# Expert blocks activated into a ring in SBUF, and latents normalised ahead of the logarithm

## The chip, the cores and the metric

The kernel runs on 1 core of one Trainium2 chip. The metric is the time of the device in microseconds (us) from start to end of one execution. A core has five engines that run side by side, each through its own queue in order: TensorE (PE, matrix products into PSUM), VectorE (DVE), ScalarE (ACT), GpSimd (POOL), and SyncE (SP), which here only issues DMAs. They wait for one another through counts (semaphores).

## The reference

Two layers of a trunk, 640 tokens (128 of context, 512 of a sample) of width 1024. What matters here, cut down:

```python
h = rmsnorm(x, norm1_g) * (1 + sc1) + sh1
(mq, mk, mv, mo, gates..., cu, cv, cq, ckv, kr) = split_cols(h @ w_in)
ml_out = ...                                   # mLSTM both ways; log_sigmoid of the forget gates
cm_out = cu * (ws @ rmsnorm(cv, cm_norm_g) + bs)          # spatial gating
q = rmsnorm(cq, mla_q_norm_g) @ mla_w_uq                   # latents, normalised
ckv_n = rmsnorm(ckv, mla_kv_norm_g)
att = attention(q, ckv_n @ mla_w_ukv, rotary keys, cached context)
x = x + g1 * (concat(ml_out, cm_out, att) @ w_out)
h2 = rmsnorm(x, norm2_g) * (1 + sc2) + sh2
# PEER: 8 heads choose 16 of 16384 single-neuron experts by product keys
act = gelu(einsum('thkd,td->thk', u_tab[eidx], h2))
x = x + g2 * einsum('thk,thkd->td', softmax(sc) * act, v_tab[eidx])
```

## The kernel before, in words

The loop over the two layers runs five stages one after the other: the input projection (`project`), the mixers (`mix`), the choice of experts (`retrieve`), the gate matrices (`gate_matrices`) and the experts (`experts`). The order on each engine is written out by hand; nothing is scheduled automatically. Products in full precision are made from a high and a low part (`_hi`, `_lo`), three passes each: ScalarE makes the high part by a copy that rounds, VectorE or GpSimd the low part by a subtraction.

**Experts.** The 640 tokens are treated in two ways. For tokens of tiles 0 and 1 the chosen rows of both tables are gathered (L1644, 1 MB each, 256 in a layer) into a ring of 6 places; VectorE takes a dot product (`dot`, L1988), ScalarE its gelu and its share (L1899, L1907), VectorE adds the weighted row (`weigh`, L1998) and frees the place (`row_used`). For the other 384 tokens all 16384 experts are computed densely in 128 blocks of 128: 116 of them (`DIRECT`) here in full, the hidden values of the last 12 earlier. For block i TensorE makes the hidden products (`hidden`, L1849, 24 matmuls) into PSUM bank i % 2, ScalarE takes the gelu in place there (L1922), VectorE multiplies by the gate block in place (`gate`, L1973), ScalarE copies the high part (`high_a`, L1913), VectorE subtracts for the low part (`low_a`, L1977), and TensorE makes the output products (`outputs`, L1860, 18 matmuls). u and v come as pairs of blocks by SP's DMAs, issued when VectorE has made u_lo (L1954, `u_split`) and v_lo (L1981, `v_split`); the gate blocks are fetched on the count `gated`.

TensorE's order is hidden(i+2), outputs(i), hidden(i+3), and so on. hidden(i+2) writes the bank of block i and so waits for `a_ready` of block i, which low_a gives; it also waits for `u_split`. VectorE's order in block i is gate(i), dots, low_u(i+2), one weigh, low_a(i), the other weighs, low_v(i), a last dot. ScalarE's is gelu(i), activations of the rows of block i-1, high_u(i+2), their shares, high_a(i), high_v(i).

**Mixers.** SP issues 3 small loads (count `rows_load`) and then 10 more (`b_load`, normg among them). VectorE first makes the gate rows r_i, r_f and r_e (L1024 to L1027), which release ScalarE's exponential and logarithm (L917, L919), then the rotary keys, then waits for `b_load` and normalises cv, cq and ckv (L1037, L1040). TensorE transposes cq and ckv (L694), ScalarE copies them (L924, L925), and then come the gating products (L701), the products of q (L710), their copies, the exponentials of the rows (L934) and the transposes of the rows into columns (L720), which VectorE copies (L1097). On VectorE the chain from the logarithm (L1044 on, scans over time) ends ahead of L1084.

**Gate matrices.** VectorE, GpSimd and ScalarE make one-hot rows by comparing `iota` with the chosen keys, TensorE multiplies them (L1712). `iota` is loaded at the start of the stage (count `e_load`), in each layer.

Of the kernel before, what the change touches and what calls it, by code (L numbers as in the profile page):

```python
# [105 lines left out]
def build_program(nc, a, o):  # L106
# [14 lines left out]
    eps_col = sb("eps_col", [P, 1])  # L121
    one_col = sb("one_col", [P, 1])
# [195 lines left out]
    with nc.Block() as block:  # L318
        @block.sync
        def _(sp):  # L320
            sp.dma_start(c_rows[:, :, :], a["c"].partition_broadcast(P)).then_inc(c_load0, 16)
            for i in range(len(FIRST) - 1):
# [12 lines left out]
            sp.wait_ge(load, 64)  # L335
# [3 lines left out]
        def _(dve):  # L339
# [11 lines left out]
            dve.wait_ge(load, 64)  # L351
# [199 lines left out]
    b_load = K.sem("b_load")  # L551
    c_load = K.sem("c_load")
# [63 lines left out]
    def mix(l):  # L616
# [29 lines left out]
        with nc.Block() as block:  # L646
            @block.sync
            def _(sp):
                sp.dma_start(cos_sin[HD:QK, :, :], a["cos_sin"]).then_inc(rows_load, 16)
                sp.dma_start(cos_sin[QK:P, 1, :], a["cos_sin"][:, 1, :]).then_inc(rows_load, 16)  # L650
                sp.dma_start(gate_b[:, :], a["gate_b"][l]).then_inc(rows_load, 16)
                loads = [(normg[:, :, :], a["normg"][l].partition_broadcast(P)), (m0[:, :], a["m0"][l]), (sel8[:, :, :], a["sel8"]),
# [29 lines left out]
            def _(pe):  # L682
# [14 lines left out]
                pe.wait_ge(b_load, 16 * 10)  # L697
# [210 lines left out]
            def _(act):  # L908
# [7 lines left out]
                act.wait_ge(nf_ready, 1)  # L916
                act.activation(r_e[:, :], r_e[:, :], ACT.Exp).then_inc(log_ready, 1)  # L917
                act.wait_ge(log_ready, 1)
                act.activation(r_e[:, :], r_e[:, :], ACT.Ln, bias=1.0).then_inc(log_ready, 1)  # L919
                act.wait_ge(b_load, 16 * 10)  # L920
                for t in range(NT):
# [5 lines left out]
                                   ACT.Copy).then_inc(lat_taken, 1)  # L927
                for h in range(AH):
# [84 lines left out]
            def _(dve):  # L1013
# [7 lines left out]
                link(dve.memset(r_m[:, :], 0.0))  # L1021
                dve.wait_ge(rows_load, 48)
# [12 lines left out]
                dve.wait_ge(b_load, 16 * 10)  # L1035
                dve.wait_ge(root15, 1)
                link(dve.reciprocal(rstd[:, 0:15], rstd[:, 0:15]))  # L1037
                for t in range(NT):
                    for i, c in enumerate((CV, CQ, CKV)):
                        ins = dve.scalar_tensor_tensor(pj(t, c), pj(t, c), rstd[:, 3 * t + i:3 * t + i + 1],  # L1040
                                                       normg[:, i, :], ALU.mult, ALU.mult)
                    ins.then_inc(normed, 1)
# [1144 lines left out]
```

## Time and profile before

| | us |
|---|---|
| median of 3 runs | 3939.42 (3938.99 to 3949.62) |
| the profiled execution, its own time | 3980.82 |
| its span | 3979.0 |
| TensorE busy | 3625.8 (91%) |
| VectorE busy | 3403.8 (86%) |
| ScalarE busy | 1483.8 (37%) |
| GpSimd busy | 1267.3 (32%) |
| mean DMA rate | 262 GB/s over the span |

Busy time is what an engine spends in instructions that the profiler records; the rest is waiting. In the profile a wait is put down to what released it last: `a <- b` says that a waited until b was done. The share of busy time is a mean over stages with different limits, so a stage has to be read for itself. The experts of the first layer lie between some 937 and 2015 us of the span, those of the second between some 2884 and 3956.

### The profile page before, as it was taken

The numbers are of one execution on the slowest core, as the hardware profiler recorded it, in microseconds if no ns is written. First come the engines' busy times: TensorE is split into PE (matmuls) and PEld (weight loads), VectorE is DVE, ScalarE is ACT, GpSimd is POOL, SyncE is SP. The second block draws the span as 40 slices with busy tenths as digits, with TensorE's granted clock in tenths as the row PEclk, the third lists the DMA queues.
The fourth block names the chain that finished last, engine by engine and source line by source line (L and its number), as shares of the span: only waits on it lengthen the run. The fifth ranks groups of instructions, "written<-read, shape, count | busy, mean of one in ns | idle before, by whom it ended". The sixth has DMA issues, their size and how long they took to land. (4 is left out here: it accounts for less than half of the span.)

```text
span 3979.0 us, 58872 instructions
## 1 busy us (share of the span) xinstructions
PE 3625.8 (91%) x19804; PEld 3185.2 (80%) x19804; DVE 3403.8 (86%) x7095; ACT 1483.8 (37%) x3422; POOL 1267.3 (32%) x1008
## 2 busy tenths in 40 slices
PE   4979989988999999999978899898889999999996
PEld 4947779667889888888778578895788888888885
DVE  8964657997999999999979557599989999999997
ACT  3331232185334343433343322323834343333343
POOL 0000023094443433444300001223934444444441
PEclk9975899999999999999989779898999999999998
DMA  6710021257999999999946101114599999999996
GB/s 243 229 60 23 1 76 59 72 211 269 405 413 414 402 403 400 403 398 399 402 142 227 43 22 54 45 47 168 194 373 399 408 406 405 406 402 400 403 411 249
DMA packets 205909, 1043.35 MB, mean 262 GB/s; under 512 B 19193, under 2 KB 74041, under 8 KB 103297
## 3 DMA queue, kind: packets, MB, share of 16 engines
q1 hardware_dynamic: 131970, 504.00, 33.3%
q0 software_dynamic: 73728, 536.90, 32.9%
q8 instruction: 88, 1.44, 0.1%
q14 instruction: 123, 1.01, 0.1%
HBM read 982.56 MB, written 58.27 MB: 262 GB/s over the span
## 5 line engine op out<-in xcount | busy, mean ns | idle before, releaser
L1644 POOL DMA_INDIRECT held_rows<-in_uv_rows,chosen x428 | 744.4, 1739 | 1169.6 <-DVE y L1998 1044.2
L1849 PE MATMUL ps<-hd_hi,u_hi 128*128 128x384 f32 x1856 | 640.8, 345 | 78.6 <-DVE a_lo L1977 67.9
L1849 PE MATMUL ps<-hd_hi,u_lo 128*128 128x384 f32 x1856 | 629.4, 339 | 0.0
L1849 PE MATMUL ps<-hd_lo,u_hi 128*128 128x384 f32 x1856 | 629.2, 339 | 0.0
L1988 DVE CUSTOM_DVE_ANT_0 held_rows<-held_rows,h2rows 128x1024 f32<-128x1024 f32 x428 | 520.7, 1218 | 67.6 <-DMA held_rows<-in_uv_rows,chosen 67.6
L1998 DVE SCALAR_TENSOR_TENSOR y<-held_rows,shares_now,y 128x1024 f32<-128x1024 f32 x428 | 545.3, 1277 | 0.0
L1899 ACT ACTIVATE acts<-dots 128x1 f32<-128x1 f32 x512 | 97.8, 195 | 1159.9 <-DVE dots L1988 1159.4
L1860 PE MATMUL ps<-v_hi,a_hi 128*128 128x512 f32 x1536 | 479.6, 394 | 14.1 <-DVE a_lo L1977 8.7
L1860 PE MATMUL ps<-v_lo,a_hi 128*128 128x512 f32 x1536 | 475.8, 391 | 0.0
L1860 PE MATMUL ps<-v_hi,a_lo 128*128 128x512 f32 x1536 | 474.8, 390 | 0.0
L1849 PEld LDWEIGHTS ps<-hd_hi,u_hi 128*128 128x128 f32 x1856 | 351.2, 189 | 119.5 <-issue 69.7
L1849 PEld LDWEIGHTS ps<-hd_lo,u_hi 128*128 128x128 f32 x1856 | 351.6, 189 | 5.1
L1849 PEld LDWEIGHTS ps<-hd_hi,u_lo 128*128 128x128 f32 x1856 | 351.5, 189 | 0.0
L1860 PEld LDWEIGHTS ps<-v_lo,a_hi 128*128 128x128 f32 x1536 | 289.8, 189 | 63.5
L1860 PEld LDWEIGHTS ps<-v_hi,a_lo 128*128 128x128 f32 x1536 | 289.7, 189 | 61.1
L1860 PEld LDWEIGHTS ps<-v_hi,a_hi 128*128 128x128 f32 x1536 | 285.5, 189 | 62.2 <-issue 15.5
L1981 DVE TENSOR_TENSOR v_lo<-v_raw,v_hi 128x1024 fp32r<-128x1024 f32 x256 | 311.9, 1219 | 12.0 <-ACT v_hi L1893 11.8
L1954 DVE TENSOR_TENSOR u_lo<-u_raw,u_hi 128x1024 fp32r<-128x1024 f32 x232 | 283.1, 1221 | 26.7 <-ACT u_hi L1888 26.7
L1893 ACT ACTIVATE v_hi<-v_raw 128x1024 fp32r<-128x1024 f32 x256 | 268.6, 1049 | 67.7 <-PE ps L1860 52.7
L1009 POOL TENSOR_TENSOR wout_lo<-wout_even,wout_hi 128x2048 fp32r<-128x2048 f32 x4 | 18.3, 4576 | 854.7 <-ACT wout_hi L989 854.7
L1712 PE MATMUL ps<-hot 128*128 128x128 f32 x1536 | 223.5, 292 | 44.8 <-POOL hot L1698 25.6
L1888 ACT ACTIVATE u_hi<-u_raw 128x1024 fp32r<-128x1024 f32 x232 | 242.7, 1047 | 37.0 <-DMA u_raw<-in_u 33.8
(316 smaller groups left out, 7448.0 us busy)
## 6 DMA issues: line engine op xcount, KB each, us to landing
v_raw<-in_v SPq DMA_DIRECT2D x128, 1024.0 KB, 9.0
u_raw<-in_u SPq DMA_DIRECT2D x116, 1024.0 KB, 13.6
mod_ring<-in_ada SPq DMA_DIRECT2D x96, 512.0 KB, 4.1
gates_dram<-gmat SPq DMA_DIRECT2D x12, 4096.0 KB, 13.7
gt<-gates_dram SPq DMA_DIRECT2D x64, 768.0 KB, 12.3
wq<-in_wq SPq DMA_DIRECT2D x8, 2048.0 KB, 8.2
ahead_raw<-in_u SPq DMA_DIRECT2D x24, 512.0 KB, 4.0
w_odd<-in_w_in SPq DMA_DIRECT2D x8, 1024.0 KB, 5.4
```

The lines of the kernel that those rows point to most:

```text
L1009: pool.tensor_tensor(wout_lo[:, c % 2, :, :], wout[c % 2], wout_hi[:, c % 2, :, :], ALU.subtract).then_inc(wout_split, 1)
L1644: pool.indirect_dma_start(picked(n).rearrange("p a d -> p (a d)"), None, a["uv_rows"], bass.IndirectOffsetOnAxis(ap=chosen[:, n % GT, n // ...
L1712: ins = pe.matmul(ps[:, q % 8, r * P:(r + 1) * P], hot2[:, s, r, :], hot1[:, s, r, :], start=True, stop=True)
L1849: ins = pe.matmul(ps[:, b % 2, 0:TD], (u_hi, u_lo)[wl][:, b % 2, k, :], (hd_hi, hd_lo)[hl][:, k, :], start=(k == 0 and n == 0), stop=(k == ...
L1860: ins = pe.matmul(ps[:, 2 + 2 * t + half, :], (a_hi, a_lo)[al][:, b % 4, t * P:(t + 1) * P], (v_hi, v_lo)[vl][:, b % 2, half * 512:(half + ...
L1888: act.activation(u_hi[:, b % 2, :, :], u_raw[:, b % 4, :, :], ACT.Copy).then_inc(u_high, 1)
L1893: act.activation(v_hi[:, b % 2, :], v_raw[:, b % 4, :], ACT.Copy).then_inc(v_high, 1)
L1899: act.activation(acts[:, i % COLS, t:t + 1], dots[:, i % COLS, t:t + 1], ACT.Gelu_apprx_tanh).then_inc(dot_act, 1)
L1954: dve.tensor_tensor(u_lo[:, b % 2, :, :], u_raw[:, b % 4, :, :], u_hi[:, b % 2, :, :], ALU.subtract).then_inc(u_split, 1)
L1981: dve.tensor_tensor(v_lo[:, b % 2, :], v_raw[:, b % 4, :], v_hi[:, b % 2, :], ALU.subtract).then_inc(v_split, 1)
L1988: dve.tensor_tensor_reduce(row, row, h2rows[:, t, :], 1.0, 0.0, ALU.mult, ALU.add, dots[:, i % COLS, t:t + 1]).then_inc(dot_ready, 1)
L1998: dve.scalar_tensor_tensor(to, picked(n)[:, 1, :], shares_now[:, i % COLS, t:t + 1], to, ALU.mult, ALU.add).then_inc(row_used, 1)
```

## The change

Three edits. (1) The gelu of a block goes from PSUM into `active`, a ring of four places in SBUF, where gate, high_a and low_a then work. The PSUM bank is free once the gelu is done, so hidden(i+2) waits for `hid_act` and no longer for `a_ready`. The rings of a_hi and a_lo shrink from four places to two, and high_a(i) waits for outputs(i-2). On ScalarE gelu(i+1) is issued in block i, ahead of the rows' activations. (2) In the mixers normg is loaded first, on a count of its own (`normg_load`), and VectorE normalises the latents ahead of the gate rows; ScalarE's exponential and logarithm stand behind its latent copies. (3) `iota` is loaded once at the start and kept; the constants eps_col and one_col share one tensor.

```diff
+    eps_one = sb("eps_one", [P, 2])
+    eps_col, one_col = eps_one[:, 0:1], eps_one[:, 1:2]
+    iota = sb("iota", [P, NKEYS])
...
+                    sp.dma_start(iota[:, :], a["iota"]).then_inc(load, 16)
...
+                sp.dma_start(normg[:, :, :], a["normg"][l].partition_broadcast(P)).then_inc(normg_load, 16)
                 sp.dma_start(cos_sin[HD:QK, :, :], a["cos_sin"]).then_inc(rows_load, 16)
...
-                loads = [(normg[:, :, :], a["normg"][l].partition_broadcast(P)), (m0[:, :], a["m0"][l]), (sel8[:, :, :], a["sel8"]),
+                loads = [(m0[:, :], a["m0"][l]), (sel8[:, :, :], a["sel8"]),
...
-                act.wait_ge(nf_ready, 1)
-                act.activation(r_e[:, :], r_e[:, :], ACT.Exp).then_inc(log_ready, 1)
-                act.wait_ge(log_ready, 1)
-                act.activation(r_e[:, :], r_e[:, :], ACT.Ln, bias=1.0).then_inc(log_ready, 1)
-                act.wait_ge(b_load, 16 * 10)
+                act.wait_ge(b_load, 16 * 9)
                 for t in range(NT):
                     act.wait_ge(lat_psum, t + 1)
...
+                act.wait_ge(nf_ready, 1)
+                act.activation(r_e[:, :], r_e[:, :], ACT.Exp).then_inc(log_ready, 1)
+                act.wait_ge(log_ready, 1)
+                act.activation(r_e[:, :], r_e[:, :], ACT.Ln, bias=1.0).then_inc(log_ready, 1)
...
-                dve.wait_ge(b_load, 16 * 10)
+                dve.wait_ge(normg_load, 16)
                 dve.wait_ge(root15, 1)
                 link(dve.reciprocal(rstd[:, 0:15], rstd[:, 0:15]))
...
-                sp.dma_start(iota[:, :], a["iota"]).then_inc(e_load, 16)
...
-    a_hi = sb("a_hi", [P, 4, TD], F32R, stack=s9)
-    a_lo = sb("a_lo", [P, 4, TD], F32R, stack=s9)
+    a_hi = sb("a_hi", [P, 2, TD], F32R, stack=s9)
+    a_lo = sb("a_lo", [P, 2, TD], F32R, stack=s9)
+    active = sb("active", [P, 4, TD], stack=s9)
...
                     if not isinstance(g, int) or g * BODY + b >= 2:
-                        pe.wait_ge(a_ready, g * BODY + b - 1)
+                        pe.wait_ge(hid_act, g * BODY + b - 1)
...
                 def high_a(g, b):
                     act.wait_ge(gated, g * BODY + b + 1)
-                    act.wait_ge(out_psum, g * BODY + b + 1)
-                    act.activation(a_hi[:, b % 4, :], ps[:, b % 2, 0:TD], ACT.Copy).then_inc(a_high, 1)
+                    act.wait_ge(out_psum, g * BODY + b + 3)
+                    act.activation(a_hi[:, b % 2, :], active[:, b % 4, :], ACT.Copy).then_inc(a_high, 1)
+
+                def gelu(i):
+                    act.wait_ge(hid_psum, i + 3)
+                    if i >= 4:
+                        act.wait_ge(a_ready, i - 3)
+                    act.activation(active[:, i % 4, :], ps[:, i % 2, 0:TD], ACT.Gelu_apprx_tanh).then_inc(hid_act, 1)
 
                 high_u(0, 0)
                 high_u(0, 1)
+                gelu(0)
                 for i in range(NKEYS):
                     g, b = i // BODY, i % BODY
                     before = rows_of(i - 1) if i >= 1 else ()
-                    if i < DIRECT:
-                        act.wait_ge(hid_psum, i + 3)
-                        act.activation(ps[:, b % 2, 0:TD], ps[:, b % 2, 0:TD], ACT.Gelu_apprx_tanh).then_inc(hid_act, 1)
-                    else:
+                    if i + 2 < DIRECT:
+                        high_u(g, b + 2)
+                    if i + 1 < DIRECT:
+                        gelu(i + 1)
+                    if i >= DIRECT:
                         high_v(g, b)
                     for n in before:
                         row_activation(n)
-                    if i + 2 < DIRECT:
-                        high_u(g, b + 2)
                     for n in before:
                         row_share(n)
                     high_a(g, b)
...
-                    to = ps[:, b % 2, 0:TD]
+                    to = active[:, i % 4, :]
```

How the order changes on ScalarE in the experts: one block of the steady part, first before, then after. u_hi is high_u of block i+2, shares_now the shares, a_hi and v_hi the high parts, and the instruction that reads ps (L1922, then L1919) the gelu.

```order
408 L1907 ACTIVATE shares_now<-acts,gates 128x1 x2
409 L1913 ACTIVATE a_hi<-ps 128x384
410 L1893 ACTIVATE v_hi<-v_raw 128x1024
411 L1922 ACTIVATE ps<-ps 128x384
412 L1899 ACTIVATE acts<-dots 128x1 x2
413 L1888 ACTIVATE u_hi<-u_raw 128x1024
```

```order
408 L1899 ACTIVATE acts<-dots 128x1 x2
409 L1907 ACTIVATE shares_now<-acts,gates 128x1 x2
410 L1913 ACTIVATE a_hi<-active 128x384
411 L1893 ACTIVATE v_hi<-v_raw 128x1024
412 L1888 ACTIVATE u_hi<-u_raw 128x1024
413 L1919 ACTIVATE active<-ps 128x384
```

Before, the gelu (L1922) stood ahead of the activations of the rows (L1899) and u_hi behind them; now u_hi and the gelu (L1919), which is that of the following block, both stand ahead of them, and with them ahead of the shares and a_hi.

On ScalarE at the start of the mixers, first before, then after; rowq is the row r_e, under L917/L919 (then L929/L931) the exponential and the logarithm, cqT and ckvT the latent copies, qT those of q.

```order
70 L917 ACT_TABLE_LOAD
71 L917 ACTIVATE rowq<-rowq 36x640
72 L919 ACT_TABLE_LOAD
73 L919 ACTIVATE rowq<-rowq 36x640
74 L924 ACTIVATE cqT<-ps 128x2x128
75 L925 ACTIVATE ckvT<-ps 128x2x128
```

```order
78 L924 ACTIVATE cqT<-ps 128x2x128
79 L925 ACTIVATE ckvT<-ps 128x2x128
80 L929 ACT_TABLE_LOAD
81 L929 ACTIVATE rowq<-rowq 36x640
82 L931 ACT_TABLE_LOAD
83 L931 ACTIVATE rowq<-rowq 36x640
84 L935 ACTIVATE qT<-ps 128x512
```

The two table loads and the two activations went from ahead of the five tiles' copies to behind them, directly ahead of the copies of q.

On VectorE at the same place, first before, then after; proj_b are the latents and cv, krT and xn the rotary keys, the first rowq rows r_i, r_f and r_e, and the last one (L1044, then L1049) the first step behind the logarithm.

```order
302 L1024 TENSOR_SCALAR rowq<-smallT,gate_b 36x640
303 L1025 TENSOR_SCALAR rowq<-smallT,gate_b 36x640
304 L1027 SCALAR_TENSOR_TENSOR rowq<-rowq 36x640
305 L1030 COPY krT<-smallT 32x128
306 L1031 TENSOR_TENSOR krT<-smallT,cos_sin 32x512
307 L1032 TENSOR_TENSOR xn<-smallT,cos_sin 32x512
308 L1033 TENSOR_TENSOR krT<-krT,xn 32x512
309 L1037 RECIPROCAL rstd<-rstd 128x15
310 L1040 SCALAR_TENSOR_TENSOR proj_b<-proj_b,rstd,normg 128x256 x15
311 L1044 SCALAR_TENSOR_TENSOR rowq<-rowq 36x640
```

```order
302 L1028 RECIPROCAL rstd<-rstd 128x15
303 L1031 SCALAR_TENSOR_TENSOR proj_b<-proj_b,rstd,normg 128x256 x15
304 L1036 TENSOR_SCALAR rowq<-smallT,gate_b 36x640
305 L1037 TENSOR_SCALAR rowq<-smallT,gate_b 36x640
306 L1039 SCALAR_TENSOR_TENSOR rowq<-rowq 36x640
307 L1042 COPY krT<-smallT 32x128
308 L1043 TENSOR_TENSOR krT<-smallT,cos_sin 32x512
309 L1044 TENSOR_TENSOR xn<-smallT,cos_sin 32x512
310 L1045 TENSOR_TENSOR krT<-krT,xn 32x512
311 L1049 SCALAR_TENSOR_TENSOR rowq<-rowq 36x640
```

The reciprocal and the fifteen normalisations went from behind the gate rows and the keys to ahead of them; the step behind the logarithm stays at row 311.

## Rows read from the trace of the kernel before

**Rows 1.** Waits of TensorE, whole span: us in total, times, longest

```profile
PE ps L1849 <- DVE a_lo L1977: 67.9, 62, 10.3
...
PE ps L694 <- DVE proj_b L1040: 13.9, 2, 7.0
```

**Rows 2.** Windows, first layer's experts: us, busy per engine, clock, DMA share, GB/s

```profile
930.00:1950.00 1020.00, 977.82 (x4873) 880.37 (x4871) 953.23 (x1210) 397.31 (x961) 411.68 (x248) 0.99 0.98 397
...
1340.00:1440.00 100.00, 98.58 (x492) 88.43 (x491) 96.36 (x123) 40.77 (x100) 39.70 (x25) 1.00 1.01 412
```

**Rows 3.** Waits of VectorE from 930 to 1950 us

```profile
DVE held_rows L1988 <- DMA held_rows<-in_uv_rows,chosen: 35.9, 29, 2.7
...
DVE u_lo L1954 <- ACT u_hi L1888: 13.6, 6, 4.5
```

**Rows 4.** Timeline, VectorE, one block: start, us, engine, line, operation

```profile
1203.58 0.56 DVE L1973 TENSOR_TENSOR ps<-ps,gt 128x384 f32<-128x384 f32 x1
...
1205.19 1.22 DVE L1954 TENSOR_TENSOR u_lo<-u_raw,u_hi 128x1024 fp32r<-128x1024 f32 x1
...
1206.32 1.27 DVE L1998 SCALAR_TENSOR_TENSOR y<-held_rows,shares_now,y 128x1024 f32<-128x1024 f32 x1
...
1207.52 0.55 DVE L1977 TENSOR_TENSOR a_lo<-ps,a_hi 128x384 fp32r<-128x384 f32 x1
...
1211.46 0.56 DVE L1973 TENSOR_TENSOR ps<-ps,gt 128x384 f32<-128x384 f32 x1
```

**Rows 5.** Timeline, TensorE, beside it: first instructions of three groups

```profile
1205.06 0.63 PE L1860 MATMUL ps<-v_hi,a_hi 128*128 128x512 f32 x2
...
1209.16 0.34 PE L1849 MATMUL ps<-hd_hi,u_hi 128*128 128x384 f32 x1
...
1213.37 0.63 PE L1860 MATMUL ps<-v_hi,a_hi 128*128 128x512 f32 x2
```

**Rows 6.** Timeline, ScalarE, the same block

```profile
1204.75 0.46 ACT L1907 ACTIVATE shares_now<-acts,gates 128x1 f32<-128x1 f32 x2
...
1206.43 0.48 ACT L1922 ACTIVATE ps<-ps 128x384 f32<-128x384 f32 x1
```

**Rows 7.** Timeline, three engines, at the first expert blocks

```profile
958.85 0.66 PE L1849 MATMUL ps<-hd_hi,u_hi 128*128 128x384 f32 x1 [10.29 <-DVE a_lo L1977]
...
963.91 1.28 DVE L1998 SCALAR_TENSOR_TENSOR y<-held_rows,shares_now,y 128x1024 f32<-128x1024 f32 x1
...
965.36 0.47 ACT L1922 ACTIVATE ps<-ps 128x384 f32<-128x384 f32 x1 [1.23 <-PE ps L1849]
```

**Rows 8.** Timeline, VectorE, at the start of the mixers

```profile
217.82 0.25 DVE L1037 RECIPROCAL rstd<-rstd 128x15 f32<-128x15 f32 x1 [2.20 <-DMA krT<-in_kr_cacheT]
...
218.11 6.03 DVE L1040 SCALAR_TENSOR_TENSOR proj_b<-proj_b,rstd,normg 128x256 f32<-128x256 f32 x15
...
224.05 0.81 DVE L1044 SCALAR_TENSOR_TENSOR rowq<-rowq 36x640 f32<-36x640 f32 x1
...
236.55 3.92 DVE L1084 SCALAR_TENSOR_TENSOR mixed<-ps,cmb,proj_b 128x64 f32<-128x64 f32 x20 [0.16 <-DVE r_u L1077]
...
264.47 0.53 DVE L1097 COPY cols<-ps 128x360 f32<-128x360 f32 x1 [5.32 <-PE ps L722]
```

**Rows 9.** Timeline, TensorE, the same stretch

```profile
219.44 5.86 PE L694 MATMUL ps<-ident,proj_b 128*128 128x128 f32 x20 [6.98 <-DVE proj_b L1040]
...
226.05 8.80 PE L701 MATMUL ps<-proj_b,wsT 128*128 128x64 f32 x40 [0.75 <-ACT ckvT L925]
```

**Rows 10.** Timeline, ScalarE, the same stretch

```profile
216.25 0.74 ACT L919 ACTIVATE rowq<-rowq 36x640 f32<-36x640 f32 x1
...
220.66 0.39 ACT L924 ACTIVATE cqT<-ps 128x256 f32<-128x256 f32 x1 [3.67 <-PE ps L694]
...
255.42 1.28 ACT L934 ACT_TABLE_LOAD   x1
```

**Rows 11.** Timeline, TensorE, at the start of the gate matrices

```profile
807.82 4.40 PE L1712 MATMUL ps<-hot 128*128 128x128 f32 x19 [9.56 <-POOL hot L1698]
```

More of the change, by code:

```diff
@@ L120, in build_program @@
     ss = sb("ss", [P, 16])
-    eps_col = sb("eps_col", [P, 1])
-    one_col = sb("one_col", [P, 1])
+    eps_one = sb("eps_one", [P, 2])
+    eps_col, one_col = eps_one[:, 0:1], eps_one[:, 1:2]
+    iota = sb("iota", [P, NKEYS])
     ps = ctx.enter_context(nc.psum_tensor("ps", [P, 8, 512], F32))
@@ L334, in _ @@
             sp.dma_start(c_dram, c_rows[0:1, :, :].rearrange("p a b -> p (a b)")).then_inc(c_stored, 16)
-            sp.wait_ge(load, 64)
+            sp.wait_ge(load, 80)
             sp.wait_ge(c_stored, 16)
@@ L350, in _ @@
             dve.wait_ge(first_mod["used"], 4 * KD)
-            dve.wait_ge(load, 64)
+            dve.wait_ge(load, 80)
             finish_modulation(dve, link, 0, normT[:, 1, :])
@@ L551, in build_program @@
     b_load = K.sem("b_load")
+    normg_load = K.sem("normg_load")
     c_load = K.sem("c_load")
@@ L696, in _ @@
                 pe.wait_ge(lat_taken, NT)
-                pe.wait_ge(b_load, 16 * 10)
+                pe.wait_ge(b_load, 16 * 9)
                 pe.wait_ge(kq_taken, NT)
@@ L1021, in _ @@
                 link(dve.memset(r_m[:, :], 0.0))
+                dve.wait_ge(normg_load, 16)
+                dve.wait_ge(root15, 1)
+                link(dve.reciprocal(rstd[:, 0:15], rstd[:, 0:15]))
+                for t in range(NT):
+                    for i, c in enumerate((CV, CQ, CKV)):
+                        ins = dve.scalar_tensor_tensor(pj(t, c), pj(t, c), rstd[:, 3 * t + i:3 * t + i + 1],
+                                                       normg[:, i, :], ALU.mult, ALU.mult)
+                    ins.then_inc(normed, 1)
                 dve.wait_ge(rows_load, 48)
@@ L1033, in _ @@
                 link(dve.tensor_tensor(krT[HD:QK, 2 * P:], krT[HD:QK, 2 * P:], turning, ALU.add))
-                dve.wait_ge(b_load, 16 * 10)
[L1036 to L1042, printed above, removed]
+                dve.wait_ge(b_load, 16 * 9)
                 dve.wait_ge(log_ready, 2)
@@ L1284, in build_program @@
     gmat = sb("gmat", [P, 2, NKEYS, GB], stack=s8)
-    iota = sb("iota", [P, NKEYS], stack=s8)
     stage = sb("stage", [P, 3, 2 * GB], stack=s8)
@@ L1617, in _ @@
                     ins.then_inc(cand_ready, 1)
-    e_load = K.sem("e_load")
     ahead, = place(75808, ("ahead", [P, AHEAD_PLACES, TD], F32))
@@ L1665, in _ @@
             def _(dve):
-                dve.wait_ge(e_load, 16)
                 dve.sem_inc(staged, 1)
@@ L1689, in _ @@
                     gather(pool, n)
-                pool.wait_ge(e_load, 16)
                 with pool.Fori(0, turns) as i:
@@ L1719, in _ @@
                 act.sem_inc(gm_stored[1], 16)
-                act.wait_ge(e_load, 16)
                 with act.Fori(0, turns) as i:
@@ L1859, in outputs @@
                             for half in range(2):
-                                ins = pe.matmul(ps[:, 2 + 2 * t + half, :], (a_hi, a_lo)[al][:, b % 4, t * P:(t + 1) * P],
+                                ins = pe.matmul(ps[:, 2 + 2 * t + half, :], (a_hi, a_lo)[al][:, b % 2, t * P:(t + 1) * P],
                                                 (v_hi, v_lo)[vl][:, b % 2, half * 512:(half + 1) * 512],
@@ L1976, in low_a @@
                     dve.wait_ge(a_high, g * BODY + b + 1)
-                    dve.tensor_tensor(a_lo[:, b % 4, :], ps[:, b % 2, 0:TD], a_hi[:, b % 4, :], ALU.subtract).then_inc(a_ready, 1)
+                    dve.tensor_tensor(a_lo[:, b % 2, :], active[:, b % 4, :], a_hi[:, b % 2, :], ALU.subtract).then_inc(a_ready, 1)
                 def low_v(g, b):
```

## Prediction, made before the changed kernel was run

> **What bounds the kernel now.** I read the waits of TensorE first. Two entries matter: 67.9 us in 62 waits before the hidden products (L1849), until VectorE has written a_lo, and 13.9 us in 2 waits before the latent transposes (L694), until proj_b is normalised [rows 1]. The change aims at both. The longest of the 62, 10.3 us, stands at the first blocks of a layer, so once in each: what repeats is 67.9 - 2 x 10.3 = 47.3 us over 232 blocks, 0.20 us a block.
>
> The windows then ask whether TensorE is the limit there. In the first layer's expert stage it is busy 977.82 of 1020 us, VectorE 953.23, and the DMA engines 0.98 of the time at 397 GB/s; the calmest 100 us have 412 GB/s at a share of 1.01, which I take for the ceiling [rows 2]. Three resources stand within 7% of each other, so the question is which one the others follow.
>
> The timelines of one block answer it. TensorE takes 1209.16 - 1205.06 = 4.10 us for the output products and 1213.37 - 1209.16 = 4.21 us for the hidden ones, 8.31 us together [rows 5]. VectorE goes from gate to gate in 1211.46 - 1203.58 = 7.88 us with two gathered rows [rows 4]. A third row, in 16 of 112 blocks, adds one more dot and one more weighing, 1.13 + 1.20 us by the spacing of passes of that size [rows 4]; the mean is 7.88 + 16/116 x 2.33 = 8.20 us. To this come VectorE's own waits: 35.9 us for gathered rows and 13.6 us for u_hi, 4.5 of it at the start [rows 3], or 45.0 / 116 = 0.39 us a block. VectorE with its waits needs 8.59 us a block, TensorE alone 8.31.
>
> So TensorE follows VectorE, and VectorE follows the gathers. No entry among VectorE's waits comes back to TensorE inside the stage: gathered rows, the load of u and v and the gate blocks are all issued on counts that VectorE gives (row_used, u_split, v_split, gated). VectorE, the gathers and the loads close a loop that does not contain TensorE; TensorE's 47.3 us are the shadow of that loop's 0.39 us a block, less what its slack absorbs.
>
> **The ring (edit 1).** It takes the wait for a_lo off the hidden products and leaves u_split and hid_act. In the block shown, a_lo ends at 1208.07 and u_lo at 1206.41, so the slack ahead of TensorE's start at 1209.16 grows from 1.09 to 2.75 us, by 1.66 us [rows 4, 5]. That is a shift, paid out once, not per block: after one or two stalls TensorE stands 1.66 us nearer to VectorE and follows its 8.59 us again. At the end of the stage the shift is lost too, since the last loads of v are issued by VectorE's counts. Value: 0; bounds -1.66 us a layer and, if the whole shift were kept at every stall, the first rival.
>
> gate, high_a and low_a now read and write SBUF. VectorE's gate on PSUM takes 0.56 and a_lo 0.55 us for 384 columns, u_lo, in SBUF alone, 1.22 us for 1024 [rows 4]. The slope inside SBUF follows from two passes of one kind: 15 normalisations of 256 columns in 6.03 us, 0.40 each [rows 8], and y, 1.20 from start to start at 1024 [rows 4]; 0.80 / 768 = 1.04 ns a column. Then u_lo cut to 384 columns would take 1.22 - 0.67 = 0.55 us: the same as on PSUM. Value 0, bounds 0 to -0.01 us on 116 gates a layer, -1 us a layer.
>
> The Trainium skill speaks for the change here (Perfetto Trace Analysis, section Optimizing Scalar/DVE Operations): an instruction of VectorE pays about 60 ns on SBUF and about 125 ns on PSUM. By that rule two instructions a block would save 0.13 us, an estimate of 15 us a layer, and since VectorE is in the loop it would count. The rows above put the difference at 0.01 us, so the sum goes by them.
>
> **The new order on ScalarE (part of edit 1).** high_u(i+2) and gelu(i+1) now stand ahead of the row shares and high_a(i). gelu(i+1) waits for hidden(i+1). Behind it in the queue are the shares, for which VectorE's weighing waits, and with it every later pass of VectorE. This is the one path from TensorE back into the loop. The price: gelu 0.41 to the next start (its 0.48 less the overlap), two short activations of about 0.11, the first share 0.28, and some 0.1 for the counts: 1.0 to 1.1 us after hidden(i+1) ends [rows 6]. In the block shown the weighing starts at 1206.32, 1.26 us after the products changed over at 1205.06 [rows 4, 5], and TensorE will be up to 1.66 us earlier still: 0 in steady state. Not at the start. There hidden(2) ends just before gelu at 965.36, and VectorE weighs at 963.91 already [rows 7]. hidden(2) can start 0.5 us earlier than 958.85, as low_a is no longer ahead of it; it ends near 964.7, the share is there at 965.7, and VectorE is 1.8 us late. The gathers and loads of these blocks are issued behind it, so the loop as a whole moves: +1.8 us a layer, bounds 0 (if the next wait for a gathered row swallows it) and +2.3 (a second such stop in the next block).
>
> **The mixers (edit 2).** normg goes first in the load queue, and VectorE normalises before the gate rows. Now it normalises from 218.11, after the reciprocal that waited until 217.82 for the last of ten loads; TensorE transposes from 219.44 and reaches the gating products at 226.05 [rows 8, 9]. With normg issued first, VectorE can begin near 211.6 to 213.5 and is done at 217.8 to 219.9. But ScalarE still waits for the other nine loads, which end at 217.8 as before. From there: copies of tiles 0 and 1 until 219.1; tile 2 can be transposed from 218.5 and, 1.22 us later (219.44 to 220.66 [rows 9, 10]), copied until 220.4; tile 4 follows two steps behind, until 222.4. The gating products start at 222.4 instead of 226.05: -3.65 us. The products of q, their copies and the exponentials whose table load stands at 255.42 follow in a row on TensorE and ScalarE and move with it.
>
> What is late next is the logarithm. ScalarE loads two tables of 1.28 us and runs two activations of 0.74 [rows 10]: 222.4 + 4.1 = 226.5, where VectorE went on at 224.05 before. Its chain of 12.5 us (224.05 to 236.55) then ends 2.4 us later. It has cover: VectorE sat idle for 5.32 us before it copied the columns at 264.47 [rows 8]. Columns 3.65 us earlier and a chain 2.4 us later leave -0.7 us if VectorE's waits for q stayed, and about +2.7 with those gone, as q comes earlier too. Value: -3.65 us a layer, bounds -4.4 and 0.
>
> **iota and the constants (edit 3).** iota is loaded once, at the start. The gate matrices no longer wait for it, but TensorE's first product there waited 9.56 us for POOL's hot rows [rows 11], and POOL makes them behind five gathers: 0, bounds 0 and -1 us a layer. One more load in the opening queue: +0.3 us once.
>
> **Sum.** 2 x (0 + 1.8 - 3.65) + 0.3 = -3.4 us. The profiled execution took 3980.8 us (span 3979.0) and would take 3977.4. It was 1% longer than the median of the runs, 3939.42; the differences carry over one to one: **3936 us**. About 0.3%, 12 us, is what a measurement of this kernel can tell from no change, so I expect none that can be told.
>
> **Rivals.**
> 1. TensorE's repeated stalls come back as time. For it: it is the busiest engine. Against: the closed loop above. Time: 3936 - 47 = 3889 us. The ceiling of DMA allows it only just: 412 against 397 GB/s is 3.6%.
> 2. VectorE's two passes on SBUF are shorter. If each of 464 lost a tenth of its 0.56 us, the loop would give back 26 us: 3910 us. This is the skill's rule as a mechanism; rows 4 and 8 speak against it.
> 3. Slower: gelu(i+1) ahead of the shares holds VectorE in ordinary blocks. It decides from the point where the share comes later than 1.26 us after hidden(i+1), the margin of the block shown. At 1.7 us VectorE could not rebuild the 0.43 us a block (8.31 - 7.88) over some three of the blocks between two three-row blocks: 16 x 1.2 = 19 us a layer, 3974 us. Against: the price of 1.1 us, and TensorE's own shift.
> 4. The mixers' gain is eaten by the later logarithm: 3936 + 7.3 = 3943 us, no change that can be told.
>
> **How the numbers follow.** My forecast has 0.60, rival 1 0.12, rival 2 0.07, rival 3 0.10, rival 4 0.11. My case alone spans 3926 to 3946 us. Rivals 1 and 2 and a tail of 0.05 of my case lie under 3927: faster 0.24. Rival 3 gives slower 0.09; same 0.67. The range must leave out no more than 0.2: from 3908, which leaves half of the first two rivals below, to 3950, above which only rival 3 stands.
>
> **What would show it.** In the profile after: no wait of L1849 for a_lo; in its place waits of the hidden products for u_lo and of the output products for v_lo, together near the old 47 us; VectorE's waits for gathered rows still near 36 us a layer; its gate and a_lo at 0.55 us; a stop of VectorE before its first weighing of about 1.8 us, for a share; the gating products and the copy of the columns each some 3.6 us earlier, counted from the start of the mixers. My prediction is wrong if TensorE's waits fall below 20 us in all, or if VectorE waits for shares in more than a few blocks.

## Result and profile after

| | before | after |
|---|---|---|
| median of 5 runs, us | 3941.31 (3938.99 to 3983.19) | 4016.36 (3974.75 to 4021.63) |
| ratio, with its interval | | 1.0117 (1.0059 to 1.0175) |
| profiled execution, span, us | 3979.0, clock 0.941 | 4014.6, clock 0.940 |
| first layer's experts, first hidden to last output product | 1077.5 | 1089.6 |
| second layer's | 1072.4 | 1095.2 |
| GpSimd busy | 1267.3 | 1353.8 |

The kernel became slower. The two profiled executions ran at the same mean clock, so their difference of 35.6 us can be read stage by stage: the two expert stages make 12.1 + 22.8 = 34.9 us of it. The attention in front of them (from the first to the last instruction that writes `prob`) takes 203 and 170 us before and 172 and 206 us after, by the clock granted there:

```profile
310.00:500.00 190.00, 179.88 (x1125) 151.08 (x1131) 122.19 (x302) 48.32 (x109) 13.76 (x3) 0.87 0.08 29
2280.00:2460.00 180.00, 173.53 (x871) 141.59 (x876) 99.59 (x270) 36.64 (x98) 0.00 (x0) 0.69 0.00 1
```

These are windows of the profile after (columns as in [rows 2]); before, the same two windows had 0.70 and 0.88. Over the profiles of all kernels the attention of a layer takes from 159 us, at a mean clock of 0.94, to 206 us, at 0.69, and sometimes neither layer has the long one (kernels 3 and 6 below). This is a large part of why single runs scatter so much. Over 105 runs of the kernel before, made beside the experiments, the time goes from 3921 to 4032 us, and it falls by some 36 us for each 0.01 of mean clock, with 6 to 7 us of scatter around that line. Below, each kernel is therefore also compared with the kernel before **at equal clock**: its runs and those of the kernel before beside it on the same chip, brought to clock 0.945 along this line. Put on it, the changed kernel lies 18 +-6 us above all 105 runs of the kernel before: the sign of 1.0117 (some 46 us) stands, but less than half of its size; the rest goes with the clock. The figures at equal clock take every run, fast or slow; from the fast ones alone they come out within 3 us of these. The two profiled executions exaggerate too: the one before lies 10 us below the line, so of their 35.6 us some 17 are scatter of single executions.

Waits of TensorE in the profile after, whole span (us, times, longest), to be read against [rows 1]:

```profile
PE ps L1849 <- DVE u_lo L1960: 81.1, 63, 9.5
...
PE ps L1860 <- DVE v_lo L1987: 21.5, 33, 2.4
...
PE ps L1860 <- DVE a_lo L1983: 8.4, 5, 3.6
```

The wait of the hidden products for a_lo is gone, and so is that of the latents for proj_b (13.9 us). But 81.1 us of waits for u_lo took the place of 67.9 us for a_lo: the new wait is longer than the old one. Waits of VectorE in the first layer's experts, against [rows 3]:

```profile
DVE held_rows L1994 <- DMA held_rows<-in_uv_rows,chosen: 34.8, 26, 2.7
...
DVE last_row L1994 <- DMA last_row<-in_uv_rows,chosen: 10.0, 8, 1.8
DVE u_lo L1960 <- ACT u_hi L1888: 14.4, 7, 4.5
DVE v_lo L1987 <- ACT v_hi L1893: 6.6, 4, 3.4
DVE y L2004 <- ACT shares_now L1907: 2.4, 2, 2.0
```

Gathered rows cost VectorE 44.8 us here and 49.7 us in the second layer; before it was 37.8 and 32.5 (held_rows and last_row together). VectorE's waits for rows, u_hi, v_hi and shares make 68.2 and 73.3 us together, against 56.8 and 52.0. The stage is 1021 us plus these waits: 1077.5 - 56.8 = 1020.7, 1072.4 - 52.0 = 1020.4, 1089.6 - 68.2 = 1021.4, 1095.2 - 73.3 = 1021.9. This is an account and no cause yet: it says that VectorE's passes cost the same in both kernels, and that the stage grew by VectorE's waits, most of all for rows (7.0 and 17.2 us). So the question is why the rows come later. GpSimd's gathers (busy, mean ns), before and after:

```profile
L1644 POOL DMA_INDIRECT held_rows<-in_uv_rows,chosen x428 | 744.4, 1739 | 1169.6 <-DVE y L1998 1044.2 <-POOLq L1355 113.6 <-issue 11.8
```

```profile
L1648 POOL DMA_INDIRECT held_rows<-in_uv_rows,chosen x428 | 811.7, 1896 | 1127.3 <-DVE y L2004 1002.0 <-POOLq L1360 113.6 <-issue 11.6
```

The mean hides two gathers of different length per block. Timeline of GpSimd before, the gathers behind the first and the second weighing of a block:

```profile
1148.10 0.94 POOL L1644 DMA_INDIRECT held_rows<-in_uv_rows,chosen  x1 [4.25 <-DVE y L1998]
1149.76 1.68 POOL L1644 DMA_INDIRECT held_rows<-in_uv_rows,chosen  x1 [0.72 <-DVE y L1998]
```

and after:

```profile
1154.27 1.01 POOL L1648 DMA_INDIRECT held_rows<-in_uv_rows,chosen  x1 [1.80 <-DVE y L2004]
1155.93 2.82 POOL L1648 DMA_INDIRECT held_rows<-in_uv_rows,chosen  x1 [0.66 <-DVE y L2004]
```

Before, the second gather took 1.68 us in 51 blocks of the first layer and 2.81 in 48 (27 and 72 in the second layer); after, 1.68 in 4 and 2.81 in 95 (7 and 92). In 15 blocks with three rows it took 4.01 us in both. VectorE's passes beside it are the same to 0.01 us. The rows that VectorE waits for are those of the long gathers: after, 33 of the 34 late rows of the first layer had a gather of 2.81 or 4.01 us, before 24 of 31. That is the lead which the experiments follow.

### The profile page after: what moved, and what is told of

Read it like the earlier page. It is cut to its first block and busy times, and to the rows that moved or that the text cites. A ratio compares the mean times of both kernels' runs of the same rounds, so it can differ in the third digit from the quotient of the medians.

```text
span 4014.6 us, 59075 instructions
## 1 busy us (share of the span) xinstructions
PE 3641.7 (91%) x19784; PEld 3197.7 (80%) x19804; DVE 3407.7 (85%) x7095; ACT 1506.5 (38%) x3422; POOL 1353.8 (34%) x1008
## 3 DMA queue, kind: packets, MB, share of 16 engines
q14 instruction: 123, 1.01, 0.1%
## 5 line engine op out<-in xcount | busy, mean ns | idle before, releaser
L1648 POOL DMA_INDIRECT held_rows<-in_uv_rows,chosen x428 | 811.7, 1896 | 1127.3 <-DVE y L2004 1002.0
L1849 PE MATMUL ps<-hd_hi,u_hi 128*128 128x384 f32 x1856 | 644.4, 347 | 82.2 <-DVE u_lo L1960 81.1
L1919 ACT ACTIVATE active<-ps 128x384 f32<-128x384 f32 x232 | 113.6, 490 | 821.6 <-PE ps L1849 821.3
## 6 DMA issues: line engine op xcount, KB each, us to landing
u_raw<-in_u SPq DMA_DIRECT2D x116, 1024.0 KB, 13.7
```

The source lines that it names most:

```text
L1648: pool.indirect_dma_start(picked(n).rearrange("p a d -> p (a d)"), None, a["uv_rows"], bass.IndirectOffsetOnAxis(ap=chosen[:, n % GT, n // ...
L1849: ins = pe.matmul(ps[:, b % 2, 0:TD], (u_hi, u_lo)[wl][:, b % 2, k, :], (hd_hi, hd_lo)[hl][:, k, :], start=(k == 0 and n == 0), stop=(k == ...
L1919: act.activation(active[:, i % 4, :], ps[:, i % 2, 0:TD], ACT.Gelu_apprx_tanh).then_inc(hid_act, 1)
```

## Experiments

Theories: **A**, gate and a_lo with all operands in SBUF lengthen the gathers (A1: it is a_lo's pass; A2: the gate's). **B**, ScalarE's order. **C**, TensorE standing closer to VectorE. **D**, the moved constants. The table holds all thirteen kernels; "second gathers" are counts of 1.68 / 2.81 us in the first layer (other lengths are named; the blocks of three rows are left out).

| | ratio of the times (interval) | us at equal clock | stages, us | second gathers |
|---|---|---|---|---|
| 1 mixers, constants only | 1.0046 (0.9999 to 1.0092) | -2.9 +-4.7 | 1072.6, 1083.0 | 55 / 44 |
| 2 SBUF, old order and old wait | 1.0069 (0.9984 to 1.0155) | +16.7 +-4.6 | 1089.7, 1083.7 | 2 / 97 |
| 3 changed, ScalarE's old order | 1.0078 (1.0019 to 1.0136) | +22.9 +-4.7 | 1081.0, 1085.0 | 8 / 91 |
| 4 PSUM, ScalarE's new order | 0.9969 (0.9920 to 1.0018) | -2.0 +-4.7 | 1071.8, 1075.2 | 69 / 30 |
| 5 gate in SBUF, a_lo from PSUM | 0.9978 (0.9941 to 1.0015) | +2.0 +-4.3 | 1078.9, 1078.0 | 45 / 54 |
| 6 gate from PSUM, a_lo in SBUF | 1.0048 (1.0008 to 1.0088) | +16.5 +-4.3 | 1088.9, 1092.2 | 4 / 95 |
| 7 a_lo behind the weighings | 1.0104 (1.0064 to 1.0145) | +24.9 +-4.3 | 1093.3, 1104.5 | see text |
| 8 = 1 and 4 together | 0.9979 (0.9938 to 1.0019) | -2.6 +-4.3 | 1075.5, 1087.8 | 35 / 64 |
| 9 half of the gathers, PSUM | 0.9835 (0.9778 to 0.9893) | -82.9 +-6.9 | 1037.3, 1039.3 | |
| 10 half of the gathers, changed | 0.9852 (0.9792 to 0.9913) | -62.5 +-6.9 | 1049.4, 1047.9 | |
| 11 = 8, gate behind the weighings | **0.9941 (0.9901 to 0.9981)** | **-29.3 +-4.6** | 1064.5, 1065.1 | 0.94, longer only in blocks of three rows |
| 12 ring, gate beside the first gather | 1.0076 (1.0038 to 1.0114) | +5.5 +-4.6 | 1083.1, 1081.1 | 81 of 3.28 |
| 13 changed, gate behind the weighings | 1.0023 (0.9976 to 1.0070) | +15.4 +-4.9 | 1082.5, 1087.8 | 95 of 3.28 |

A single profile's stage scatters by some 10 us between the layers of one kernel, so both layers are best taken together. With a_lo on PSUM and the old place of the gate (before, kernels 1, 4, 5, 8) the two stages make 2147 to 2163 us and VectorE's waits for rows 57 to 74 us; with a_lo in SBUF (after, 2, 3, 6) 2166 to 2185 us and 86 to 95 us. The two groups do not overlap, and their means lie 22 us apart. Inside the first group the share of long second gathers goes from 29 to 72 of 99 without the stages following it, so the length of a gather alone does not tell the time.

**Which edit (1 to 4).** Kernel 1 is the changed one with edit 1 undone. Kernel 2 is the kernel before with this (the rings of a_hi and a_lo shrink with it as in the change, and high_a waits for outputs(i-2)):

```diff
-  act.activation(ps[:, b % 2, 0:TD], ps[:, b % 2, 0:TD], ACT.Gelu_apprx_tanh)
+  act.activation(active[:, i % 4, :], ps[:, i % 2, 0:TD], ACT.Gelu_apprx_tanh)
-  to = ps[:, b % 2, 0:TD]
+  to = active[:, i % 4, :]                # the gate; a_hi and a_lo likewise
```

Kernel 3 is the changed kernel with ScalarE's loop in the old order, kernel 4 the kernel before with the loop in the new one.

> Only edits 2 and 3 (latents normalised first, iota loaded once); activated blocks stay in PSUM and ScalarE keeps its order. Measures: the expert stage, from the first hidden product to the end of the last output product, took 1077.1 and 1072.1 us in the kernel before and 1089.3 and 1094.8 us in the changed one; the mean gather on GpSimd 1739 and 1896 ns. Theory A (the loss lies in edit 1 and there in VectorE's passes on SBUF, which lengthen the gathers): expert stages 1075 +-5 us, held_rows gathers 1.74 us, time about 7 us under the kernel before. Theory B (the loss lies in edit 1, by ScalarE's order): the same. Theory D (the moved iota and constants shift the experts): expert stages near 1092 us here already, time 20 to 35 us above the kernel before.

> The kernel before with the activated blocks in SBUF: gelu writes to the ring, the gate, a_hi and a_lo read there. ScalarE's order is the old one and the hidden products still wait for a_lo. Theory A: gathers 1.90 us, VectorE's waits for gathered rows 45 to 50 us a layer, expert stages 1085 to 1095 us. Theory B (ScalarE's order): gathers may lengthen, but the rows' waits stay at 33 to 38 us a layer and the stages at 1075 +-5 us. Theory C (TensorE standing closer to VectorE, as its hidden products no longer wait for a_lo): as B, 1075 us.

> The changed kernel with ScalarE's old order (gelu of block i at the head of block i, high_u between the row activations and the shares). Theory A: no better than the changed kernel, stages 1088 to 1095 us, gathers 1.90 us. Theory B: stages back at 1075 +-5 us, with VectorE's waits for rows at 33 to 38 us a layer. Theory C: stages 1088 to 1095 us.

> The kernel before with ScalarE's new order alone: high_u(i+2) and gelu(i+1) ahead of the row activations, shares and a_hi; the blocks stay in PSUM and the hidden products wait for a_lo. Theory A: gathers 1.74 us, stages 1075 +-5 us (up to 1.8 us more a layer at the first blocks). Theory B: stages 1088 to 1095 us, VectorE waits for shares or rows 10 to 20 us more a layer. Theory C: 1075 us.

The place decides. Kernels 2 and 3 lose 17 and 23 us, with the old order and, in kernel 2, with the old wait for a_lo; kernels 1 and 4 lose nothing that can be told. B, C and D fall. Kernel 2's VectorE waited for rows 45.3 and 43.0 us. Kernel 3's stages are less bad than A asked for (1081 and 1085), its time is not. The gathers of kernels 1 and 4 came out shorter than forecast, 1.58 to 1.65 us in the mean, and kernel 1's second stage, 1083.0 us, longer than its 1075 +-5.

**Which pass (5 and 6).** Both are the changed kernel with one of the two passes led back to PSUM:

```diff
 # 5: the gate reads the ring and writes to PSUM, where a_hi (not shown) and a_lo read
-  to = active[:, i % 4, :]
+  to = ps[:, b % 2, 0:TD]
-  hidden = to
+  hidden = active[:, i % 4, :]
-  dve.tensor_tensor(a_lo[:, b % 2, :], active[:, b % 4, :], a_hi[:, b % 2, :], ALU.subtract)
+  dve.tensor_tensor(a_lo[:, b % 2, :], ps[:, b % 2, 0:TD], a_hi[:, b % 2, :], ALU.subtract)
 # 6: gelu in place in PSUM (not shown)
-  hidden = to                             # the gate reads the ring
+  hidden = ps[:, b % 2, 0:TD]             # it reads PSUM and writes the ring
```

> So far: an expert stage lasts 1021 us plus VectorE's waits in all twelve stages seen, and with the activated blocks in SBUF the gathers on GpSimd take 1.89 us in the mean against 1.58 to 1.78; the gather behind a block's second weighing takes 2.81 us nearly always, where it takes 1.68 us in about half of the blocks with PSUM. This kernel is the changed one, but the gate reads the ring and writes to PSUM, and a_hi and a_lo read PSUM (the hidden products wait for a_lo again). Theory A1 (a_lo's pass, which runs beside the gather behind the first weighing, is what counts when all its operands lie in SBUF): half of the second gathers at 1.68 us again, mean 1.65 +-0.1, VectorE's waits 50 to 60 us a layer, time at equal clock within 5 us of the kernel before less the mixers' 3 us. Theory A2 (the gate's pass counts): second gathers at 2.81 us, mean 1.89, waits 62 to 72 us, 15 to 20 us above the kernel before at equal clock.

> The reverse: gelu writes to PSUM in place, the gate reads PSUM and writes the ring in SBUF, a_hi and a_lo read the ring. The hidden products wait for the gate instead of a_lo, so that this is also a way to take their wait off a_lo with one pass less in SBUF alone. Theory A1: second gathers at 2.81 us nearly always, mean 1.85 to 1.91, waits of VectorE 62 to 72 us a layer, 15 to 20 us above the kernel before at equal clock. Theory A2: half of the second gathers at 1.68 us, waits 50 to 60 us a layer, within 5 us of the kernel before.

Gathers in kernel 6, then in kernel 5 (mean ns of all):

```profile
L1648 POOL DMA_INDIRECT held_rows<-in_uv_rows,chosen x428 | 813.8, 1901 | 1121.3 <-DVE y L2002 996.0 <-POOLq L1360 113.6 <-issue 11.6
```

```profile
L1648 POOL DMA_INDIRECT held_rows<-in_uv_rows,chosen x428 | 726.3, 1697 | 1171.0 <-DVE y L2004 1045.6 <-POOLq L1360 113.6 <-issue 11.8
```

A1 holds as forecast: it is a_lo, the pass that stands beside the first gather. The gate in SBUF does no harm that can be told in the place it has. The two kernels have the same buffers, so neither the ring's place in SBUF nor the shorter rings of a_hi and a_lo are the cause. One thing goes with a_lo in all of these kernels: ScalarE's copy a_hi reads the same place as a_lo. No run takes the two apart, but the traces speak against a_hi. In none of the 2.81 us gathers of the profile after and of kernels 2, 3 and 6 does an a_hi run before the last 0.9 us, and in kernels 2 and 3 ScalarE does nothing at all until then. And in kernel 12 below a_hi reads SBUF too, and the first gather, with a PSUM pass of VectorE beside it, takes 0.94 us.

**Around it (7 to 10).** Kernel 7 is the changed one with a_lo moved behind all weighings; kernel 8 joins 1 and 4; 9 and 10 gather only the even rows.

> The changed kernel with VectorE's a_lo moved behind all weighings of a block, so that it no longer stands between the first gather's issue and the second's; the second weighing and its gather come 0.47 us earlier. Both theories: VectorE's row waits fall by about the 0.47 us in the blocks where a row is late (some 30 a layer, -10 to -14 us a layer) if the second gather's length stays; if the two gathers now follow within 1.2 us and the second one only queues behind the first on GpSimd, nothing changes. TensorE waits for a_lo ahead of its output products are possible, since a_lo ends 1.2 us later than now, but v_lo ends later still: 0. I expect 5 to 20 us less than the changed kernel at equal clock.

> The two parts that did no harm together: edits 2 and 3, and ScalarE's new order, with the activated blocks left in PSUM. Measured apart at equal clock: -3.1 +-4.5 us and -1.8 +-4.5 us. Together 3 to 7 us under the kernel before, stages 1072 to 1078 us, gathers 1.58 to 1.65 us. If the small gain of the order was chance, -3 us.

> Edits 2 and 3 with the activated blocks in PSUM, and every second gather left out after the first six: the rows with an odd number are read from what lies in their place, so y is not the reference's. VectorE does the same passes. It is the partner of the next kernel. Stage so far = 1021 us plus VectorE's waits. Without half of the gathers: waits for rows near 0, stages 1035 to 1050 us.

> The changed kernel with every second gather left out in the same way. Theory A (edit 1 loses its time through the gathers alone): stages within 3 us of the partner's, instead of 14 to 29 us in both layers together above the kernels with PSUM. Theory E (the activated blocks in SBUF cost something by themselves, in VectorE's passes or TensorE's reads): the stages stay 7 to 10 us each above the partner's. Theory C' (TensorE's freed wait is worth something once the gathers are out of the way): 3 to 8 us each under the partner's, as TensorE alone needs 116 x 8.31 + 12 x 4.1 = 1013 us and VectorE 1021.

Kernel 7 is a miss: it lies 7 +-7 us above the changed kernel, where I expected 5 to 20 below. The second weighing did come earlier, but not its gather, for the first one now has a weighing beside it and takes longer:

```profile
1236.72 1.74 POOL L1648 DMA_INDIRECT last_row<-in_uv_rows,chosen  x1 [2.96 <-DVE y L2004]
1238.76 1.30 POOL L1648 DMA_INDIRECT held_rows<-in_uv_rows,chosen  x1 [0.30 <-issue]
```

1.74 us in place of 1.01, and 2.40 in the mean of the first layer's blocks with two rows. There the second gather starts 1.78 us after its weighing in place of 0.29, queued behind the first. Kernel 8 gains no more than either of its parts could, and is in part a miss: its gathers take 1.69 and 1.73 us in the mean of a layer and its second stage 1087.8 us, both above the forecast. The pair 9 and 10 is a miss too: the stages with SBUF stay 12.1 and 8.6 us longer, where A allowed 3, and where E asked for 7 to 10. (The pair differs also in ScalarE's order, old in kernel 9, new in 10.) The windows from 1000 to 1900 us of kernel 9 and of kernel 10 say why that figure was wrong:

```profile
1000.00:1900.00 900.00, 898.30 (x4538) 819.47 (x4538) 886.06 (x1124) 369.58 (x893) 259.58 (x116) 1.00 0.73 282
```

```profile
1000.00:1900.00 900.00, 893.71 (x4498) 813.31 (x4497) 881.24 (x1116) 369.30 (x885) 272.01 (x115) 1.00 0.72 280
```

The DMA engines are down to 0.73, and still VectorE waits for rows, 13.9 and 14.9 us in kernel 9, 20.9 and 19.8 us in kernel 10. Every row that it waits for there had a gather of 2.3 us or more on GpSimd, and took 8.6 to 8.7 us in the mean from the gather's end to its landing, where all rows take 6.5 to 6.8. So the late issue stays and a lower load does not cure it. VectorE's waits (rows, v_hi, shares) differ by 10.1 and 6.4 us, most of the stages' difference; some 2 us a layer lie outside them, so E is not excluded for that much, though gate and a_lo are no longer in kernel 10 (565 and 561 ns) than in kernel 9 (579 and 567). C' falls as well: TensorE, now busy 898 of 900 us, gains nothing by the ring.

**The mechanism turned to use (11 to 13).** Kernel 11 is kernel 8 with one pass moved on VectorE, so that each of the two gathers has a pass on PSUM beside it; kernel 13 is the same move in the changed kernel, where both passes lie in SBUF and the hidden products wait for gelu in place of a_lo; kernel 12 is kernel 6 with the gate in a_lo's place and a_lo behind the weighings.

```diff
   for i in range(NKEYS):
-      gate(g, b)
+      if i == 0: gate(0, 0)
       ...
       for n in before[1:]:
           weigh(n)
+      if i + 1 < NKEYS: gate((i + 1) // BODY, (i + 1) % BODY)
```

> Edits 2 and 3, ScalarE's new order, blocks in PSUM, and VectorE's gate of block i+1 moved from the head of its block to right behind the last weighing of block i, so that a pass on PSUM stands beside the second gather as a_lo stands beside the first. Theory A1 as a mechanism (a pass of VectorE on PSUM lets GpSimd finish the gather beside it): second gathers near 0.94 us in place of 1.68 or 2.81, VectorE's waits for rows down from some 32 to 15 to 22 us a layer, 15 to 30 us less than the kernel without the move at equal clock. Rival: what lies beside the second gather does not matter, only the first one's: its length stays at 1.68 or 2.81 and the time within 5 us; if VectorE now waits for gelu at the gate, up to 10 us more.

> The ring without a pass in SBUF beside the first gather: gelu stays in PSUM, the gate of block i+1 (PSUM to the ring) takes the place between the first two weighings, and a_lo (in SBUF) goes behind the last one. The hidden products wait for the gate only. Theory A1: first gather 0.94 us, and the second at 1.68 in half of the blocks; stages at 1075 to 1085 us, within 6 us of the kernel before at equal clock less the mixers' gain. If a_lo in SBUF beside the second gather hurts as much as beside the first: second gathers 2.81 us, stages 1088 to 1095 us, as in the changed kernel.

> The changed kernel with VectorE's gate of block i+1 right behind the last weighing of block i: the order of the kernel that gained 27 us at equal clock, but gate and a_lo read and write SBUF alone. Theory A1 (what counts is a pass on PSUM beside the gather): first gathers 1.01 us, second ones no shorter than 2.81 us, stages 1085 to 1100 us, 15 to 25 us above the kernel before at equal clock, so some 45 us behind its twin with PSUM. Theory F (the order is what gained): second gathers still long, but the stages fall by the same 17 us a layer as in the twin's case against the kernel with the changed order of ScalarE in PSUM, and the time lies at or below the kernel before at equal clock.

Timeline of GpSimd in kernel 11, then in kernel 13:

```profile
1242.81 0.94 POOL L1647 DMA_INDIRECT last_row<-in_uv_rows,chosen  x1 [6.06 <-DVE y L2001]
1244.47 0.94 POOL L1647 DMA_INDIRECT held_rows<-in_uv_rows,chosen  x1 [0.72 <-DVE y L2001]
```

```profile
1155.16 1.01 POOL L1648 DMA_INDIRECT last_row<-in_uv_rows,chosen  x1 [2.94 <-DVE y L2004]
1156.83 3.28 POOL L1648 DMA_INDIRECT held_rows<-in_uv_rows,chosen  x1 [0.65 <-DVE y L2004]
```

The same order on VectorE, the same lengths of its passes; with the gate on PSUM the second gather takes 0.94 us, in SBUF 3.28. At equal clock the twins lie 29.3 + 15.4 = 45 us apart. Kernel 11 has 43.9 us of VectorE's waits in each layer, 18.8 and 16.1 of them for rows:

```profile
DVE held_rows L1991 <- DMA held_rows<-in_uv_rows,chosen: 18.8, 24, 1.7
DVE u_lo L1957 <- ACT u_hi L1887: 14.6, 12, 4.5
```

Kernel 11 beats both kernels: 0.9941 of the time before. Theory F falls: kernel 13 has the same order and loses 15 us. Its first stage, 1082.5 us, is below the forecast 1085 to 1100. Kernel 12 lies between: its first gather is at 0.94 us and its second, beside a_lo in SBUF, at 3.28, a length that neither theory named, and it loses 5.5 us. Which share of that belongs to which gather was not taken apart. Nor is the time a matter of the length alone: the 3.28 us of kernel 13 cost no more than the 2.81 us of the changed kernel (95 and 94 us of waits for rows in both layers).

What the lengths are can be read from the traces, laid over VectorE's passes. A gather of 1.68 or 2.81 us ends 0.88 to 0.90 us after the start of a pass of VectorE: all 78 of 1.68 us in the profile before after the first start that falls into them, all 120 of 2.81 us there and all 187 in the profile after after the second one. The first gathers of 1.01 us do the same (0.89 to 0.91 us after the first start, 236 of 236), only that this start comes 0.11 or 0.12 us behind their own; the 0.94 us ones end 0.81 to 0.83 us after it. 2.81 - 1.68 = 1.13 us is so the step from one pass of 1024 columns to the next, and most of the 3.28 us gathers take the third start, 3.28 - 2.81 = 0.47 us being the step of the gate. Why a gather lets a start go by is open: it does so in 29 to 72 of 99 blocks of a layer with a_lo on PSUM and in 91 to 97 with a_lo in SBUF, though a_lo has ended before the second gather begins. Something of the first gather may still hold GpSimd when the second comes; no run shows it.

The Trainium skill (SBUF — State Buffer, section Who interferes with whom) has the rule that fits: a VectorE instruction with two SBUF inputs contends with a GpSimd instruction that reads SBUF, one with at most one SBUF input, outside its two-port modes, does not. The pairs 5 and 6, 11 and 13 agree (mean gather 1.70 against 1.90 us, second gather 0.94 against 3.28 us). The same section describes the contention as an exclusive lock and reports that `tensor_tensor` was not seen to hold up a DMA that GpSimd issues; here it does, 3.28 against 0.94 us.

## Why the prediction was wrong

**The step that failed** is the price of the passes in SBUF: "gate, high_a and low_a now read and write SBUF ... Value 0, bounds 0 to -0.01 us on 116 gates a layer". The passes themselves cost what I said, the gate 555 ns after and 560 before, a_lo 552 and 550:

```profile
L1983 DVE TENSOR_TENSOR a_lo<-active,a_hi 128x384 fp32r<-128x384 f32 x128 | 70.7, 552 | 0.0
L1979 DVE TENSOR_TENSOR active<-active,gt 128x384 f32<-128x384 f32 x116 | 64.3, 555 | 14.4 <-DMA gt<-gates_dram 14.4
```

But I priced them on their own engine alone and gave no bound for what GpSimd does beside them. The gathers' two lengths stood in the trace of before, and I had placed the gathers in the loop that sets the time; I did not ask what in VectorE's passes made one 1.68 and the next 2.81 us long. In its place the runs show, with a_lo's pass in SBUF, second gathers of 2.81 us in 95 of 99 blocks, waits for rows of 94.5 us in both layers in place of 70.3 (I had them staying near 36 us a layer), and +16.7 and +22.9 us for the whole (kernels 2 and 3). That it is a_lo's pass kernels 5 and 6 show: +2.0 and +16.5 us.

**The loop without TensorE** held: 1021 us plus VectorE's waits gives the stage within 4 us in every kernel (1019.8 to 1024.5 us in the fixed part with all gathers, 1018 to 1020 with half). Edit 1 freed TensorE of its wait for a_lo and that was worth nothing (kernel 3, which has edits 2 and 3 too, lies 6 +-7 us above kernel 2: no gain). Rival 1 falls. I forecast that the waits for u_lo and v_lo would be near 47 us in place of a_lo's; they are 102.6. Of these 13.7 us stood in the profile before already, and VectorE's waits for rows grew by 24 us.

**ScalarE's order** was put at +1.8 us a layer, with waits for shares only at the first blocks. They came (2.4 and 3.8 us), but kernel 4, with 6.2 and 8.1 us of them, shows -2.0 +-4.7 us for both layers: no cost that can be told. Rival 3, my slower case, named this as the cause; that the kernel became slower came true by another mechanism, so that rival was right by luck. Rival 2, shorter passes on SBUF, falls with the rows above.

**The mixers** did what was worked out. From the first product of the mixers to the gating products, before [rows 9] and after:

```profile
208.66 0.45 PE L687 MATMUL ps<-ident,proj_a 128*128 128x128 f32 x1 [9.41 <-PEq L394]
```

```profile
210.62 0.44 PE L691 MATMUL ps<-ident,proj_a 128*128 128x128 f32 x1 [9.71 <-PEq L396]
...
224.33 6.02 PE L705 MATMUL ps<-proj_b,wsT 128*128 128x64 f32 x27 [0.75 <-ACT ckvT L925]
```

226.05 - 208.66 = 17.4 us before, 224.33 - 210.62 = 13.7 after: -3.7 against -3.65. The copy of the columns came at 55.8 us [rows 8] and comes at 50.9, 4.9 us earlier where 3.6 was forecast (the rest was not taken apart):

```profile
261.54 0.53 DVE L1102 COPY cols<-ps 128x360 f32<-128x360 f32 x1 [1.24 <-PE ps L726]
```

VectorE's cover of 5.32 us shrank to 1.24, so the later logarithm did not eat the gain (rival 4). As a time it is -2.9 +-4.7 us with the constants (kernel 1), which neither confirms nor denies the -7 us forecast.

My range of 3908 to 3950 us also took the first three runs for the kernel's spread; the median of its 105 runs is 3981. Even so the sum was wrong by more than that: -3.4 us forecast against +18 +-6 at equal clock.

## What to carry to other kernels

When a change moves operands from PSUM to SBUF, price it on the neighbours too: where GpSimd issues indirect DMAs, list what VectorE runs beside each, and keep a pass with an input in PSUM there; putting the two such passes of this loop beside its two gathers was worth 27 +-6 us (kernel 11 against 8). A buffer ring that removes the longest wait of the busiest engine is worth nothing if another engine's loop sets the pace, and it can cost if it changes where that engine reads. Where the clock scatters by per cents, compare runs at equal clock, and stages inside the profile, before explaining a ratio.

## What the runs showed of the hardware

- An indirect gather of 128 rows took GpSimd 0.94 us where a VectorE pass with one input in PSUM ran when it began. Where the passes read both inputs from SBUF it took mostly 1.01, 1.68, 2.81 or 3.28 us (4.01 or 4.47 in blocks of three rows), and nearly always ended 0.88 to 0.91 us after the start of a VectorE pass: the first, the second or the third that fell into it.
- Rows came late even where the DMA engines were busy only 0.73 of the time, all of them rows whose gather took 2.3 us or more (kernels 9 and 10).
- VectorE's pass over 384 columns took the same time with an input in PSUM or all in SBUF: 0.56 and 0.55 us.
- The granted clock in the attention of a layer lay between 0.69 and 0.94 from profile to profile; 0.01 of the mean clock is some 36 us of this kernel.
